# Gate/up of the experts as three fp32r products of split parts, and expert rows added to token rows in DRAM

## The chip, the cores and the metric

The kernel runs on one core of a Trainium2 chip. The time is device microseconds of one execution. PE is TensorE, DVE VectorE, ACT ScalarE, POOL GpSimd and SP SyncE, which issues most of the transfers.

## What is computed

Two layers of a trunk over 384 tokens (128 context, 256 latent) of 1024 features. The part that matters here is the mixture of experts at the end of each layer: each token picks 4 of 32 experts, and their outputs are added with its weights, beside one shared expert.

```python
def moe(h, lp):
    t = h.reshape(B * T, D)
    ...
    _, eidx = lax.top_k(masked, TOP_K)
    w = jnp.take_along_axis(scores, eidx, axis=-1)
    w = w / jnp.sum(w, axis=-1, keepdims=True) * ROUTE_SCALE
    combine = jnp.sum(jax.nn.one_hot(eidx, N_EXPERTS, dtype=jnp.float32) * w[..., None], axis=1)
    gu = jnp.einsum('nd,edf->nef', t, lp['w_exp_gu'])
    a = jax.nn.silu(gu[..., :EXPERT_FF]) * gu[..., EXPERT_FF:]
    a = (a * combine[..., None].astype(a.dtype)).reshape(-1, N_EXPERTS * EXPERT_FF)
    routed = a @ lp['w_exp_down'].reshape(N_EXPERTS * EXPERT_FF, D_MODEL)
    ...
    return (routed + shared).reshape(B, T, D)
```

Each expert has gate/up weights of 1024 x 512 (2 MB in fp32) and down weights of 256 x 1024 (1 MB).

## The kernel before

A layer runs through modulation, input projection, four mixers, gates and output projection, and then the experts. The large projections already use split parts (`project_split`, L1809): ACT writes a weight piece rounded to fp32r (L1001), DVE writes the rest (L1338, the piece minus its rounded part), and three fp32r products of 512 columns take the place of one fp32 product (L1822).

The experts work on tiles of CAP = 96 slots, one tile for each expert and further ones for experts with more than 96 tokens; with these inputs it is 32 tiles a layer, in 16 turns of two. Routing on DVE gives each of a token's four choices a slot; POOL scatters token numbers into a table in DRAM (L894) and reads it back. The token rows lie in DRAM (`token_rows`).

The loop has two slots, e = 0 and 1, and each engine runs its own `steps(turn)`; semaphores alone order them. PE's step for tile n (L2078): `gate_up` of tile n+1 (L2059, 8 fp32 products into one PSUM bank, through the helper line L1762), `turn_product` of tile n (L2013), `turn_gathered` of tile n+2 (L2052, eight transposes of gathered rows) and `down` of tile n (L2018, four fp32 products). ACT takes the SiLU (L1238), the transposed product (L1240), half of the transposed rows (L1244) and half of the output rows (L1248); DVE takes the product (L1669), the other half of the transposed rows (L1732) and of the output rows (L1735). The two slots' weights lie in W.

SP's step (L738): when `gate_up` has filled its bank, load the 2 MB of gate/up weights of tile n+3 into the slot just used; when `down` is done, load 1 MB of down weights of tile n+2; when both halves of the output rows are copied, write them to `y_slots` in DRAM (`write_rows`, L725). POOL's step (L916): when the rows of tile n+2 are transposed, copy the index column of tile n+4 (L904) and issue an indirect gather of its rows (L907).

After the loop POOL gathers, for each of a token's four choices, the rows of `y_slots` by slot (L927, twelve gathers of 128 rows a layer), DVE multiplies each by the token's weight and adds it to the shared expert's output `acc` (L1744), ACT takes the sum of squares and its root (`row_root`, L1173) and DVE the residual (`residual`, L1572). The slots of tiles that may not run are zeroed beforehand by POOL (L871, 96 x 16 rows of 4 KB).

Of the kernel before, what the change touches and what calls it, by code (L numbers as in the profile page):

```python
# [189 lines left out]
def plan_jobs():  # L190
# [100 lines left out]
    for i in range(2):  # L291
        for h in range(2):
            jobs.add(("xt", i, h), ("act", "dve")[h], BANK_XT + h)
# [17 lines left out]
STEP = (("gu", "dve"), ("aT", "act"), ("xt0", "act"), ("xt1", "dve"), ("y0", "act"), ("y1", "dve"))  # L311
TURN_JOBS, TURN_TAKEN = 2 * len(STEP), 6
# [37 lines left out]
def trunk(nc, a):  # L350

    J = JOBS
    with ExitStack() as ctx:
# [3 lines left out]
        def sb_twice(name, n):  # L357
# [54 lines left out]
                 "do_ready", "gate_ready", "merged_ready", "m_squared", "x_ready", "exp_ready", "chosen_ready", "slots_ready", "ones_ready", "gathers", "sp_steps", "sil_ready", "mod_params_in", "table_reset", "slots_out", "table_in", "rows_out", "tables_ready", "summed", "silu_ready",  # L412
                 "mod_used", "mod_rows_out", "modT_in", "lam_dots", "lam_exps", "head_normed", "mean_ready", "ret_squared", "branch_rs"]
        names += ["gates_in", "cache_out"] + [f"{n}{i}" for n in ("x_landed", "y_written", "index_copied") for i in range(2)]
        names += [f"y_landed{i}" for i in range(6)]
        names += ["dec_scaled", "mixture_rows", "post_root", "pre_root", "zeros_ready", "zeros_out", "halves_used", "high_ready", "low_ready", "h_split", "oT_high", "mgT_high"]
        landed_names = [f"piece_landed{i}" for i in range(RAW)] + ["gu_landed0", "gu_landed1", "dn_landed0", "dn_landed1"]
# [77 lines left out]
        xT = zf[:, 9728:9728 + 2 * KD * CAP].rearrange("p (s k n) -> p s k n", s=2, k=KD)  # L495
        yrow = zf[:, 11776:13824].rearrange("p (s n) -> p s n", s=2)
        ybuf = zf[:, 7680:13824].rearrange("p (s n) -> p s n", s=6)

        slot_f, weight, slot_u = vm[:, 1024:1036], vm[:, 1036:1048], vm[:, 1048:1060].bitcast(U32)
        token_f, token_u = vm[:, 1060:1063], vm[:, 1063:1066].bitcast(U32)  # L500
        tokens = vm[:, 1068:1068 + NT].bitcast(U32)
        index = vm[:, 1120:1122].bitcast(U32)
        expert_f, expert_u = vm[:, 1124:1124 + NT], vm[:, 1172:1172 + NT].bitcast(U32)
        turns_f, turns_u = vm[:, 1220:1221], vm[:, 1221:1222].bitcast(U32)
        ones = vm[:, 1232:1360]
# [29 lines left out]
        def expert_gu(s):  # L535
            return W[:, s * SLOT:(s + 1) * SLOT].rearrange("p (k n) -> p k n", k=KD)

# [132 lines left out]
        with nc.Fori(0, DEPTH) as l:  # L670
            with nc.Block() as block:

                @block.sync
                def _(sp):
# [24 lines left out]
                    def load_gate_up(s, src):  # L699
                        sp.dma_start(expert_gu(s), src.rearrange("(p k) n -> p k n", p=P)).then_inc(S[f"gu_landed{s}"], 16)  # L700
# [1446 lines left out]
```

## Time and profile before

| | us |
|---|---|
| median of 3 runs | 2185.84 (2184.77 to 2186.19) |
| the profiled execution | 2186.99 |
| its span | 2185.4 |
| PE busy in the span | 1951.3 (89%) |
| DVE busy | 832.7 (38%) |
| ACT busy | 628.2 (29%) |
| POOL busy | 318.8 (15%) |
| mean granted clock of PE | 0.953 of 2.4 GHz |

The profile is one execution. Matmuls overlap, so a busy PE is not a PE at its peak. DMA figures are those of the core's 16 DMA engines together: a share of 1 means that packets were in service on all of them all the time. The chain that ended last is 40% PE work, of which L1762 has 19% of the span and L1822 17%; DMA has 2%.

### The profile page before, as it was taken

The numbers are of one execution on the slowest core, as the hardware profiler recorded it, in microseconds if no ns is written. First come the engines' busy times: TensorE is split into PE (matmuls) and PEld (weight loads), VectorE is DVE, ScalarE is ACT, GpSimd is POOL, SyncE is SP. The second block draws the span as 40 slices with busy tenths as digits, with TensorE's granted clock in tenths as the row PEclk, the third lists the DMA queues.
The fourth block names the chain that finished last, engine by engine and source line by source line (L and its number), as shares of the span: only waits on it lengthen the run. The fifth ranks groups of instructions, "written<-read, shape, count | busy, mean of one in ns | idle before, by whom it ended". The sixth has DMA issues, their size and how long they took to land.

```text
span 2185.4 us, 24671 instructions
## 1 busy us (share of the span) xinstructions
PE 1951.3 (89%) x8272; PEld 1236.6 (57%) x8272; DVE 832.7 (38%) x1468; ACT 628.2 (29%) x1318; POOL 318.8 (15%) x381
## 2 busy tenths in 40 slices
PE   6998988999978999999169989989999789999990
PEld 3886656888753444444048866578887434444440
DVE  2345566444462111111523455664444521111115
ACT  3342357333340111111133423573232401111111
POOL 2004121300012011100210051223000121001102
PEclk9999998999999999999679999999999999999995
DMA  8442360734345999998375424617333569999974
GB/s 299 139 134 93 119 230 16 243 122 135 116 183 199 341 350 349 345 345 303 131 264 155 121 87 137 212 34 242 124 117 114 189 218 345 345 345 351 347 276 159
DMA packets 110956, 457.60 MB, mean 209 GB/s; under 512 B 11984, under 2 KB 19824, under 8 KB 87824
## 3 DMA queue, kind: packets, MB, share of 16 engines
q1 hardware_dynamic: 87168, 384.86, 50.7%
q0 software_dynamic: 20192, 65.15, 10.0%
q10 hardware_dynamic: 3504, 6.40, 0.8%
q8 instruction: 54, 0.88, 0.2%
q14 instruction: 38, 0.31, 0.0%
HBM read 411.69 MB, written 44.71 MB: 209 GB/s over the span
## 4 chain that ended last, share of the span: by engine, by line
PE 40%; DVE 4%; DMA 2%; ACT 2%; issue 1%; POOL 1%; SPq 0%; ACTq 0%; POOLq 0%; DVEq 0%
PE psum L1762 19%; PE psum L1822 17%; PE psum L1769 2%; PE psum L1787 1%; PE psum L2055 1%; DMA W<-in_w_mod 1%; POOL slot_tokens L894 1%; DVE W_split L1338 0%; DVE zf L1744 0%; DVE zf L1577 0%; DMA zf<-token_rows,vm 0%; DMA W<-in_w_in 0%; ACT hT L970 0%; DMA zf<-y_slots,vm 0%; PE psum L2015 0%
## 5 line engine op out<-in xcount | busy, mean ns | idle before, releaser
L1762 PE MATMUL psum<-W,zf 128*96 128x512 f32 (+1 forms) x1584 | 699.5, 597 | 9.5 <-issue 4.3
L1762 PEld LDWEIGHTS psum<-W,zf 128*96 128x96 f32 (+1 forms) x1584 | 254.3, 164 | 403.6 <-issue 388.8
L1822 PE MATMUL psum<-W_split,qT_split 128*128 128x512 f32 (+3 forms) x1536 | 405.7, 377 | 9.9 <-ACT hT L970 7.8
L1338 DVE TENSOR_TENSOR W_split<-W,W_split 128x2048 fp32r<-128x2048 f32 (+3 forms) x96 | 225.1, 2346 | 406.3 <-ACT W_split L1001 406.3
L1822 PEld LDWEIGHTS psum<-W_split,qT_split 128*128 128x128 f32 x1536 | 284.8, 190 | 60.3 <-ACT hT L970 8.6
L1001 ACT ACTIVATE W_split<-W 128x2048 fp32r<-128x2048 f32 (+3 forms) x96 | 176.0, 1839 | 414.6 <-PE psum L1822 343.0
L1822 PE MATMUL psum<-W_split,scratch_split 128*128 128x512 f32 x864 | 274.7, 390 | 0.6 <-DVE hT_split L1333 0.6
L1822 PE MATMUL psum<-W_split,hT_split 128*128 128x512 f32 x576 | 208.9, 390 | 5.8 <-DVE scratch_split L1536 5.8
L1669 DVE TENSOR_TENSOR zf<-psum,zf 96x256 f32<-96x256 f32 x64 | 26.9, 421 | 425.9 <-ACT zf L1238 410.3
L1822 PEld LDWEIGHTS psum<-W_split,scratch_split 128*128 128x128 f32 x864 | 161.6, 188 | 34.1 <-DVE hT_split L1333 0.8
L1822 PE MATMUL psum<-W_split,kT_split 128*128 128x512 f32 (+3 forms) x480 | 176.4, 367 | 0.0
L1238 ACT ACTIVATE zf<-psum 96x256 f32<-96x256 f32 x62 | 23.6, 380 | 494.7 <-PE psum L1762 494.7
L1787 PE MATMUL psum<-W,silT 128*32 128x512 f32 x384 | 66.5, 767 | 69.5 <-DMA W<-in_w_mod 69.4
L1822 PEld LDWEIGHTS psum<-W_split,hT_split 128*128 128x128 f32 x576 | 107.9, 188 | 28.8 <-DVE scratch_split L1536 6.3
L1735 DVE COPY zf<-psum 96x512 f32<-96x512 f32 x64 | 44.0, 687 | 201.4 <-PE psum L1762 201.4
L1822 PEld LDWEIGHTS psum<-W_split,kT_split 128*128 128x128 f32 x480 | 91.8, 191 | 13.3
L904 POOL COPY vm<-vm 96x1 uint32 (+1 forms) x64 | 11.5, 180 | 556.3 <-PE psum L2055 553.4
L1414 DVE TENSOR_REDUCE nmax<-psum 128x1 f32<-128x128 f32 (+1 forms) x144 | 64.6, 463 | 46.6 <-PE psum L1762 46.0
L1769 PE MATMUL psum<-const,zf 128*128 128x128 f32 x372 | 56.2, 292 | 29.1 <-DVE zf L1585 19.3
L1762 PE MATMUL psum<-kT,qT 64*128 64x384 f32 (+3 forms) x288 | 75.0, 485 | 5.1 <-DVE kT L1275 1.8
L877 POOL DMA_DIRECT2D kT<-mod_rows x8 | 4.4, 548 | 470.4 <-PE psum L1769 346.1
L1769 PEld LDWEIGHTS psum<-const,zf 128*128 128x128 f32 x372 | 47.2, 159 | 45.1 <-DVE zf L1585 20.2
(306 smaller groups left out, 2050.4 us busy)
## 6 DMA issues: line engine op xcount, KB each, us to landing
W<-in_w_exp_gu SPq DMA_DIRECT2D x64, 2048.0 KB, 9.8
W<-in_w_exp_down SPq DMA_DIRECT2D x64, 1024.0 KB, 8.6
W<-in_w_in SPq DMA_DIRECT2D x60, 1024.0 KB, 5.1
W<-in_w_mod SPq DMA_DIRECT2D x48, 1024.0 KB, 4.9
y_slots<-zf SPq DMA_DIRECT2D x64, 384.0 KB, 8.7
W<-in_w_br SPq DMA_DIRECT2D x16, 1024.0 KB, 5.1
y_slots<-kT POOLq DMA_DIRECT2D x2, 6144.0 KB, 33.6
W<-in_w_out SPq DMA_DIRECT2D x8, 1024.0 KB, 5.0
```

The source lines that it names most:

```text
L894: pool.indirect_dma_start(a["slot_tokens"], bass.IndirectOffsetOnAxis(ap=slot_u[:, i:i + 1], axis=0), token_u[:, i // TOPK:i // TOPK + 1], ...
L1001: nc.scalar.activation(high(j), piece(SPLITS[j]), ACT.Copy).then_inc(S["high_ready"], 1)
L1238: nc.scalar.activation(silu[0:CAP, 1 - e, :], psum[0:CAP, BANK_GU + 1 - e, 0:FF], ACT.Silu).then_inc(S["silu_ready"], 1)
L1338: V.tensor_tensor(piece(SPLITS[j], Wr), piece(SPLITS[j]), high(j).bitcast(F32), ALU.subtract).then_inc(S["low_ready"], 1)
L1414: V.tensor_reduce(nmax[:, col:col + 1], bank(key, P * len(keys_of(t))), AX, ALU.max, negate=True).then_inc(S["max_ready"], 1)
L1669: V.tensor_tensor(av[0:CAP, s], psum[0:CAP, gu, FF:2 * FF], silu[0:CAP, s], ALU.mult).then_inc(S["dve_emptied"], 1)
L1735: V.tensor_copy(yrow[0:CAP, e, C:], psum[0:CAP, BANK_Y + 1, :]).then_inc(S["dve_emptied"], 1)
L1762: ins = nc.tensor.matmul(dst, lhsT, rhs, start=(i == 0), stop=(i == len(pairs) - 1))
L1769: ins = nc.tensor.transpose(psum[0:n, J.bank(key), i * P:(i + 1) * P], src, ident)
L1787: ins = nc.tensor.matmul(bank(("mod", j), C, slice(32 * q, 32 * q + 32)), silTv[:, k, :], chunk, start=k == 0, stop=k == KD - 1)
L1822: ins = nc.tensor.matmul(bank(job, piece_size(key)[1]), act_part[:, k0 + k, t * P:(t + 1) * P], w_part[:, k, :], start=first and (k, i) == ...
L2055: ins = nc.tensor.transpose(psum[:, BANK_XT + h, k * CAP:(k + 1) * CAP], xg[0:CAP, s, (4 * h + k) * P:(4 * h + k + 1) * P], ident[0:CAP, 0 ...
```

## The change

Gate/up weights come in two halves of 1 MB, each with its own semaphore (`gu_landed` for slot and half). ACT rounds each half to fp32r into one of two buffers (`gate_up_high`, one for each half, shared by both slots), DVE overwrites the half in W with the rest, and PE multiplies rows and weights in three fp32r products for each of the 8 blocks of features. The gathered rows are split too: ACT writes both rounded halves of the transposed rows, DVE both rests. SP loads half 0 of a slot as soon as PE has used half 0, and half 1 at the end of `gate_up`. PE's order is unchanged: `gate_up` of the next tile, `turn_product`, `turn_gathered`, `down`.

The table in DRAM has two words for each slot, token number and weight; DVE's product multiplies by the slot's weight, so output rows leave the loop weighted. The shared expert's rows are written to `y_sums` in DRAM, and POOL adds each tile's 96 output rows to the rows of their tokens by an indirect transfer with addition, one tile after the other: it waits for each to land. Empty slots point to 96 rows behind the tokens'. After the loop SP loads `y_sums` back, and the roots and residuals follow; gathers and sums by choice are gone, and so is the zeroing of `y_slots`.

```diff
-STEP = (("gu", "dve"), ("aT", "act"), ("xt0", "act"), ("xt1", "dve"), ("y0", "act"), ("y1", "dve"))
+STEP = (("gu", "dve"), ("aT", "act"), ("xt0", "dve"), ("xt1", "dve"), ("y0", "act"), ("y1", "dve"))
+AHEAD = 8
...
+                    sp.wait_ge(*emptied(("y", "s", T - 1, 1)))
+                    sp.dma_start(a["y_sums"][0:T * P].rearrange("(t p) n -> p t n", p=P), acc).then_inc(S["shared_out"], 16)
...
                             if not (last and e == 1):
+                                sp.wait_ge(S["gu_half_used"], AHEAD + 2 + tile)
+                                weights = expert("w_exp_gu", expert_of(tile + 3))
+                                load_gate_up(1 - e, weights, (0,))
                                 sp.wait_ge(*job_filled(turn, e, "gu"))
-                                load_gate_up(1 - e, expert("w_exp_gu", expert_of(tile + 3)))
+                                sp.sem_inc(S["sp_steps"], 1)
+                                load_gate_up(1 - e, weights, (1,))
                             sp.wait_ge(*job_filled(turn, e, "y1"))
                             load_down(e, expert("w_exp_down", expert_of(tile + 2)))
-                            write_rows(turn, e)
...
+                    def add_rows(turn, e, less=(0, 0)):
+
+                        pool.wait_ge(*job_emptied(turn, e, "y0", less[0]))
+                        pool.sem_inc(S["gathers"], 1)
+                        pool.wait_ge(*job_emptied(turn, e, "y1", less[1]))
+                        pool.sem_inc(S["gathers"], 1)
+                        nc.gpsimd.tensor_copy(sum_index[0:CAP, e:e + 1], of_tile(turn * 2 + e, 0).bitcast(U32)).then_inc(S["sum_index_copied"], 1)
+                        pool.wait_ge(S["sum_index_copied"], turn * 2 + e + 1 + AHEAD)
+                        pool.sem_inc(S["gathers"], 1)
+                        pool.indirect_dma_start(a["y_sums"], bass.IndirectOffsetOnAxis(ap=sum_index[0:CAP, e:e + 1], axis=0),
+                                                yrow[0:CAP, e, :], None, compute_op=ALU.add).then_inc(S["y_added"], 16)
+                        pool.wait_ge(S["y_added"], turn * 32 + 16 * e + 16)
+                        pool.sem_inc(S["rows_added"], 1)
...
+                    def steps(turn, more, less=((0, 0), (0, 0))):
                         for e in range(2):
+                            if more != "none":
+                                pool.wait_ge(*job_filled(turn, e, "xt1"))
+                                if more == "rows":
+                                    gather(turn * 2 + e + 4, e, turn + 3)
+                                else:
+                                    pool.sem_inc(S["gathers"], 1)
+                                weights_of(turn * 2 + e + 2, e)
+                            add_rows(turn, e, less[e])
...
                     def steps(turn, last=False):
                         for e in range(2):
+                            if not last:
+                                act.wait_ge(S[f"gu_landed{e}0"], turn * 16 + 32 + 16 * e)
+                                act.wait_ge(S["gu_half_used"], turn * 2 + e + 2 + AHEAD)
+                                weights_high(e, 0)
...
+                                act.wait_ge(*job_filled(turn, e, "xt1"))
+                                rows_high(e)
+                                act.wait_ge(S[f"gu_landed{e}1"], turn * 16 + 32 + 16 * e)
+                                weights_high(e, 1)
                             act.wait_ge(*job_filled(turn, e, "y0", LESS["y"][e] if last else 0))
-                            act.wait_ge(S[f"y_written{e}"], turn * 16 + 16)
+                            act.wait_ge(S["rows_added"], turn * 2 + e - 1 + AHEAD)
...
+                    def weights_low(s, h, waited):
+                        dve.wait_ge(S["gu_high"], waited + h + 1)
+                        V.tensor_tensor(gate_up_half(s, h, Wr), gate_up_half(s, h), gate_up_high[h].bitcast(F32), ALU.subtract).then_inc(S["gu_low"], 1)
...
-                    for i in range(T * TOPK):
-                        dve.wait_ge(S[f"y_landed{i % 6}"], 16 * (i // 6 + 1))
-                        V.scalar_tensor_tensor(acc[:, i // TOPK], ybuf[:, i % 6], weight[:, i:i + 1], acc[:, i // TOPK], ALU.mult,
-                                               ALU.add).then_inc(S["summed"], 1)
...
+                    for t in range(T):
+                        residual(acc, 1, t)
...
+                    def gate_up(s, waited):
+
+                        for h in range(2):
+                            pe.wait_ge(S["gu_low"], waited + h + 1)
+                            parts = [(xT_split[a], (gate_up_high[h], gate_up_half(s, h, Wr))[b]) for a, b in ((0, 0), (0, 1), (1, 0))]
+                            for k in range(4):
+                                for i, (rows_part, w_part) in enumerate(parts):
+                                    ins = nc.tensor.matmul(psum[0:CAP, BANK_GU + s, :], rows_part[:, s, 4 * h + k, :], w_part[:, k, :],
+                                                           start=(h, k, i) == (0, 0, 0), stop=(h, k, i) == (1, 3, 2))
+                            ins.then_inc(S["gu_half_used" if h == 0 else "psum_filled"], 1)
```

## Rows read from the trace of the kernel before

**Rows 1.** The page, 40 equal slices of the span, busy share in tenths.
```profile
PE   6998988999978999999169989989999789999990
...
DMA  8442360734345999998375424617333569999974
```

**Rows 2.** Windows: us, each engine's busy us (count), granted clock, DMA share, GB/s.
```profile
11.00:16.00 5.00, 4.08 (x16) 0.43 (x16) 0.17 (x1) 4.66 (x8) 0.00 (x0) 1.00 1.01 418
403.00:437.00 34.00, 34.00 (x157) 28.29 (x156) 12.80 (x12) 10.46 (x11) 1.48 (x3) 1.00 0.90 299
1900.00:1990.00 90.00, 90.00 (x268) 38.28 (x268) 12.72 (x23) 12.15 (x30) 8.83 (x16) 1.00 1.01 346
1906.00:1910.00 4.00, 4.00 (x11) 1.52 (x10) 0.00 (x0) 0.00 (x0) 0.00 (x0) 1.00 1.01 282
1913.00:1917.00 4.00, 4.00 (x11) 1.50 (x10) 0.69 (x1) 0.59 (x1) 0.25 (x1) 1.00 1.00 375
1764.00:1786.00 22.00, 17.20 (x49) 7.58 (x50) 1.48 (x4) 1.38 (x4) 2.03 (x3) 0.85 0.46 150
2134.80:2172.10 37.30, 0.00 (x0) 0.00 (x0) 28.41 (x24) 5.62 (x10) 15.16 (x12) 0.56 0.53 179
```

**Rows 3.** Chain of waits, second layer: start us, us, what.
```profile
1180.13 98.26 PE psum L1822 x432
...
1809.01 10.53 PE psum L1762 x24
1819.54 0.20 PE psum L2015 x2
1819.74 0.66 PE psum L2055 x8
1820.40 10.44 PE psum L1762 x24
```

**Rows 4.** Groups by line and shape, whole run: busy us, mean ns, idle before.
```profile
L1338 DVE TENSOR_TENSOR W_split<-W,W_split 128x2048 fp32r<-128x2048 f32 x84 | 207.7, 2475 | 357.5 <-ACT W_split L1001 357.5
...
L1001 ACT ACTIVATE W_split<-W 128x2048 fp32r<-128x2048 f32 x84 | 161.1, 1925 | 339.1 <-PE psum L1822 304.5 <-DMA W<-in_w_in 20.4 <-DMA W<-in_w_br 14.2
...
L1244 ACT ACTIVATE zf<-psum 128x384 f32<-128x384 f32 x60 | 29.5, 491 | 0.0
```

**Rows 5.** DMA, 1900 to 1990 us: queues (packets, MB, share), gathers (median us to landing).
```profile
q1 hardware_dynamic: 3161, 28.02, 88.1%
q0 software_dynamic: 892, 3.14, 12.9%
...
zf<-token_rows,vm POOLq DMA_INDIRECT x8, 10.6
```

**Rows 6.** Timeline of POOL: one step of a gather.
```profile
1763.81 0.18 POOL L904 COPY vm<-vm 96x1 uint32<-96x1 uint32 x1 [2.99 <-PE psum L2055]
1764.80 0.92 POOL L907 DMA_INDIRECT zf<-token_rows,vm  x1 [0.80 <-POOL vm L904]
```

**Rows 7.** The tile token_rows: its transfers from issue to landing.
```profile
DMA to landing us min/median/max: 2.7/10.2/11.2
```

**Rows 8.** Timeline of the second layer's end.
```profile
2134.78 0.69 DVE L1735 COPY zf<-psum 96x512 f32<-96x512 f32 x1 [3.58 <-PE psum L1762]
...
2151.16 1.06 ACT L1173 ACTIVATE zf<-zf 128x1024 f32<-128x1024 f32 x1 [17.50 <-DVE zf L1744]
...
2153.62 0.29 ACT L1174 ACTIVATE rs<-stat,const 128x1 f32<-128x1 f32 x1
...
2154.51 0.16 DVE L1576 RECIPROCAL rs<-rs 128x1 f32<-128x1 f32 x1
...
2156.03 1.22 DVE L1578 TENSOR_TENSOR x<-x,zf 128x1024 f32<-128x1024 f32 x1
...
2170.83 1.22 DVE L1578 TENSOR_TENSOR x<-x,zf 128x1024 f32<-128x1024 f32 x1
```

**Rows 9.** DMA issues of the whole run: KB each, median us to landing.
```profile
x<-in_x_prompt ACTq DMA_DIRECT2D x1, 512.0 KB, 3.9
```

More of the change, by code:

```diff
@@ L750, in _ @@
                     steps(turns - 2, last=True)
-                    for e in range(2):
-                        write_rows(turns - 1, e, (LESS["act"][e], LESS["dve"][e]))
+                    sp.wait_ge(S["rows_added"], turns * 2 + AHEAD)
+                    sp.sem_inc(S["sp_steps"], 1)
+                    for t in range(T):
+                        sp.dma_start(acc[:, t], a["y_sums"][t * P:(t + 1) * P, :]).then_inc(S[f"y_landed{t}"], 16)
                 @block.gpsimd
@@ L870, in _ @@
                     pool.wait_ge(S["zeros_ready"], 1)
-                    pool.dma_start(a["y_slots"].rearrange("(p i) n -> p i n", i=NT)[:, NE:, :],
-                                   zero_row[0:CAP, None, :].to_broadcast([CAP, NT - NE, D])).then_inc(S["zeros_out"], 16)
+                    for name in ("token_rows", "y_sums"):
+                        pool.dma_start(a[name][T * P:, :], zero_row[0:CAP]).then_inc(S["zeros_out"], 16)
                     def fetch_gates(n):
@@ L901, in gather @@
                     def gather(tile, e, n):
[L903 to L904 removed]
+                        nc.gpsimd.tensor_copy(index[0:CAP, e:e + 1], of_tile(tile, 0).bitcast(U32)).then_inc(S[f"index_copied{e}"], 1)
                         pool.wait_ge(S[f"index_copied{e}"], n)
@@ L2020, in down @@
                                  ).then_inc(S["psum_filled"], 1)
-                    pe.wait_ge(S["gu_landed1"], 16)
+                    for h in range(2):
+                        pe.wait_ge(S[f"gu_landed1{h}"], 16)
                     def shared_gate_up(t):
@@ L2080, in steps @@
                             before = previous(turn, e)
-                            gone = (1 if last and e == 1 else 0)
+                            gone = (2 if last and e == 1 else 0)
                             if not (last and e == 1):
@@ L2093, in steps @@
                                 turn_gathered(e)
-                            pe.wait_ge(*job_emptied(turn, e, "aT", LESS["act_aT"][e] if last else 0))
+                            pe.wait_ge(*job_emptied(turn, e, "aT"))
                             pe.wait_ge(S[f"dn_landed{e}"], turn * 16 + 16 * (e + 1))
-                            pe.wait_ge(*job_emptied(*before, "y0", gone))
+                            pe.wait_ge(*job_emptied(*before, "y0"))
                             down(BANK_Y, aT[:, e], e, 0, CAP)
```

171 lines of the change are left out of this document (99 added, 72 removed).

## Prediction

> **What bounds the kernel now.** I read the page by slices first [rows 1]: PE is at 9 tenths in both expert loops (slices 14 to 18 and 34 to 38 of 40), DMA is at 9 tenths in the same slices, and nowhere else do both stand at 9 for long. The windows say it sharper [rows 2]: in 1900 to 1990 us PE is busy 90.00 of 90.00 us at a granted clock of 1.00 (the 2.4 GHz level), DVE 12.72 and ACT 12.15 us, and the DMA share is 1.01 at 346 GB/s. The chain of waits [rows 3] gives the tile: 24 records of L1762 in 10.53 us (8 of `down`, then 16 of `gate_up`: an fp32 product of 512 columns is two records of 0.44 us), 0.20 us for `turn_product`, 0.66 us for `turn_gathered`, and the next group 11.39 us later (11.30 from the other slot), 11.35 us on average. PE waits for nothing in the loop, so PE sets the pace. But the second resource has no room: a tile moves 2.10 MB of gate/up weights, 1.05 MB of down weights, 0.39 MB of gathered rows and 0.39 MB of written rows, 3.93 MB, and 3.93 MB in 11.35 us is the 346 GB/s of the window. The engines can do better when only weight loads run (418 GB/s in 11 to 16 us), and do worse while gathered rows are mixed in (282 GB/s in 1906 to 1910, against 375 in 1913 to 1917) [rows 2]. So shortening PE's part of a tile helps only as far as DMA can follow.
>
> **Gate/up in three products.** Removed: 16 records, 16 x 0.44 = 7.0 us. Added: 24 fp32r matmuls of 512 columns. The projections of the mixers run this form: 432 in 98.26 us, 0.227 us each [rows 3]. 24 x 0.227 = 5.5 us, so PE's tile would be 11.35 - 1.55 = 9.8 us. The stationary tile has 96 instead of 128 columns; I take no difference.
>
> The parts must be made. ACT copies two halves of 128x2048 (1.925 us each) and one more row copy (0.49), DVE subtracts two halves (2.475 each) and one more row half (about the same half microsecond) [rows 4]. Per tile ACT now has 12.15 x 11.35/90 = 1.5 us and DVE 1.6 us [rows 2], so they come to 5.9 and 7.1 us; both fit beside a tile of 9.8 us. Their latency is on the path once per half, since one high buffer per half serves both slots: from the end of `gate_up` of one tile, half 1 of the next needs `turn_product` and `turn_gathered` (0.86), two row copies (0.98), the high part (1.93) and the low part (2.48), 6.3 us before waits, while PE does the transposes (0.86), `down` (3.5) and half 0 (2.7), 7.1 us. That just hides; if it didn't, the excess would be added to each tile (a lower bound of about 10.0 us for a tile, by my estimate of some 0.1 us for each hand-over). Cover gone, the price is 1 us a tile for each us of delay. Before the loop the first splits stand beside the wait for the tables and the gathered rows; the larger table, the two extra DVE operations and the row split cost about a microsecond a layer, the first and last `gate_up` give about as much back: zero, 3 us either way.
>
> **Rows added in DRAM.** Removed from each tile: SP's write of 0.39 MB. Added: a POOL issue of the same size that adds to rows of y_sums. No row shows an adding transfer. As a plain write it would change nothing, since those bytes still leave the core; less than nothing it could cost only if POOL's queue moved rows faster than SP's, and it doesn't. In 1900 to 1990 the write's queue moved 28.02 MB in 88.1% of the window, 353 GB/s, and POOL's queue, which holds the gathers alone, 3.14 MB in 12.9%, 270 GB/s [rows 5]. The write is then worth 1.1 us of all engines and a gather 1.46 us. An add must fetch the token's row, as a gather does, and write one, as the write does: 2.57 us, 1.46 more than now. In bytes: 0.39 MB more, 4.32 MB a tile, at 346 GB/s 12.5 us. The upper end: the mixed rate. At 282 mixed and 375 unmixed, 11.35 us for 3.93 MB holds 3.5 us of mixing a tile; POOL's queue would carry three times as much (0.39 gathered, 0.79 for the add), 10.5 us at 282 and the last 1.36 MB at 375: 14.1 us. The lower end: all 4.32 MB at the 418 GB/s of pure loads, 10.3 us. I take 12.5, the value by the loop's own rate, since the loop is the nearest row.
>
> The window shows the share at 1.01 with nothing to spare, so a second read per added byte must lengthen the tile [rows 2]. The Trainium skill has a rule that speaks against the change here (Collectives: The Full Stack, The bandwidth ceiling: the fold count and why AG ≠ RS ≠ AR): a transfer that adds costs twice a copy, because it reads two sources on the same ring, and the addition itself is free. By that rule the add is two reads and the tile 12.5 us; by the write's row alone it is a copy and the tile stays at 11.35 us or less. No run here shows which.
>
> The new waits. POOL waits for each add to land (`y_added`) before anything else. Behind that wait stand the next gather and the next weight copy; PE's `turn_gathered` and DVE's product wait for those, and ACT's and DVE's copies into yrow wait for `rows_added` of two tiles before. A POOL step is: index copy 0.18, 0.80 of wait, gather issue 0.92 [rows 6], weight copy 0.2, index copy and wait 1.0, then issue to landing of the add. Gathers land after 10.6 us in the loaded loop [rows 5] and 2.7 us at best [rows 7], so a step is 3.1 + 2.7 = 5.8 to 3.1 + 10.6 = 13.7 us. In a 12.5 us tile it decides from a landing of 9.4 us on. Weight packets of half the size let POOL's rows in more often, so I keep it just below, and as a rival. SP loses the waits for y0 and y1 and its write, and issues half 0 of the weights some 2.7 us sooner; both only fill the same engines earlier.
>
> Full steps with loads behind them are about 28 a layer (the first ones start with DMA at a share of 0.46 [rows 2], the last three load nothing), 56 in all: 56 x (12.5 - 11.35) = +64 us.
>
> **The end of a layer.** From the last yrow copy (2134.78) to the last residual (2172.05) are 37.3 us: write, twelve gathers through POOL, twelve weighted sums on DVE [rows 8]. After: copy 0.7, POOL 1.0, add 5 (between a gather's best 2.7 [rows 7] and twice that; nearer the second, as it reads and writes), hand-over 0.5 by my estimate, a 512 KB load 3.9 [rows 9], root 2.8 (2151.16 to 2153.91), three residuals of 2.74 (2154.51 to 2157.25), 8.2: 22 us [rows 8]. That is 15 saved; an earlier add still ahead of it would leave 8; I take 13, 26 in both layers. The zero fill of y_slots (6 MB a layer) goes too; it lay beside PE's projections, busy 34.00 of 34.00 us from 403 to 437 [rows 2], so I give it nothing. The 1.5 MB of shared rows written to y_sums fall in the stretch with a DMA share of 0.46 [rows 2]: nothing, and 4 us at 375 GB/s a layer if that cover is gone.
>
> **Sum.** The profiled execution took 2186.99 us (span 2185.4, and 1.6 around it); the median of the runs, 2185.84, is 1.15 lower. 2187 + 64 - 26 = 2225, as a median 2224 us. The rivals below start from the median. The change breaks even at a tile of 11.35 + 26/56 = 11.8 us.
>
> **Rivals.** B, faster: DMA follows. For it: 418 GB/s without gathered rows; halves issued earlier keep the queue from running dry; a share of 1.01 may hide packets that merely wait. Against: 9.8 us would need 441 GB/s counted with two reads, more than [rows 2] has anywhere; even with the add as a plain write it needs 401. Tiles of 10.3 us give 2186 + 56 x (-1.05) - 26 = 2101; PE's and the splits' own 10.0 us 2084; the end of it is 11.8 us, 2185.
>
> C, slower still: POOL's serial order decides. The add stands in POOL's queue behind a gather issued 2 us before, so its landing holds what is left of that one too. At a landing of 10.6 us the tile is 13.7: 2186 + 56 x 2.35 - 20 = 2298. For it: the loaded landing of 10.6 [rows 5]. Against: 2.7 at best [rows 7], smaller weight packets, and a longer tile unloads the engines. At the mixed rate's 14.1 us: 2186 + 154 - 20 = 2320.
>
> D, PE waits so long in each tile that its clock falls to the lower level, 1.2 GHz: PE's part doubles to 19.6 us, some 2620 us. The clock was 0.56 in the layer's end, when PE did nothing for 37 us, but 1.00 through the loop [rows 2]; waits of 2 to 3 us per tile are far from the former. That three products aren't shorter than one (the change not doing what it says) has 432 matmuls against it [rows 3]; with DMA as the bound it would hardly move the time, and stands in the forecast.
>
> **Chances.** Forecast A (tile of 11.8 to 13.3 us, 2185 to 2270): 0.48. B: 0.36. C: 0.13. D: 0.03. Range 2095 to 2310: it reaches into B down to a tile of 10.2 us and into C past its 2298, leaving out about 0.1 below and 0.1 above. A's own range is 2185 to 2270. A measurement of this kernel can tell some 0.2%, 4.4 us, from no change; around the break-even tile that is 0.08 us either way, 0.04. So faster 0.35, same 0.04, slower 0.61.
>
> **What would show it.** In the loop: DMA share still at 1, PE below 90% with idle time ended by DVE's low parts or ACT's copies that in turn wait for a load or for `rows_added`; tile period near 12.5; the fp32r records at 0.227 us; POOL's adds landing in 8 to 9 us, bytes per tile 4.3 MB. PE busy 100% with a share below 1 would prove B; POOL idle only for `y_added` with a share well below 1 would prove C. In the layer's end: some 24 us instead of 37. Wrong it would be above all if an adding packet takes no longer than a plain one, or far longer than a gather and a write together.

## The result, and the profile after

| | kernel before | changed kernel |
|---|---|---|
| median of the runs, us | 2186.02 (2184.77 to 2188.36) | 2227.52 (2225.41 to 2232.79) |
| profiled execution / its span, us | 2186.99 / 2185.4 | 2226.58 / 2225.0 |
| a tile, mean of 30 between copies into yrow, us | 11.35 | 12.44 |
| last copy into yrow to last residual, us | 37.3 | 26.0 |

The changed kernel is slower by 1.8%: 1.0184 times the time of before, 95% interval 1.0165 to 1.0202. The forecast was 2224 us. The time came out as forecast, and most terms of the sum did too; the mechanism under the largest term was another, the one I had kept as rival C. That is the subject of the experiments.

First the page of the changed kernel (the slices that answer to [rows 1], the chain that ended last).

```profile
PE   6998988999977888898469989889998778888883
...
DMA  8442461433367999999475424514432589999994
...
PE psum L1900 16%; DMA y_sums<-zf,vm 10%; PE psum L1840 4%; PE psum L2145 2%; PE psum L1847 2%; PE psum L1865 1%; DMA W<-in_w_mod 1%; POOL slot_tokens L908 1%; POOL vm L938 1%; DMA zf<-token_rows,vm 0%; DVE W_split L1400 0%; POOL vm L920 0%
```

In the expert loops (slices 14 to 19 and 34 to 39) PE has fallen from 9 tenths to 8, but for one slice; DMA still stands at 9. And a transfer that did not exist before, `y_sums<-zf`, the adding of rows, holds 10% of the chain, second only to the mixers' projections. A window in the second loop gives the sizes (columns as in [rows 2]).

```profile
1800.00:2000.00 200.00, 170.21 (x673) 101.15 (x674) 105.01 (x98) 92.05 (x113) 48.44 (x75) 0.96 0.96 314
```

The DMA queues and issues of the same window (columns as in [rows 5]):

```profile
q1 hardware_dynamic: 7097, 51.72, 71.3%
q0 software_dynamic: 3136, 11.01, 24.7%
...
zf<-token_rows,vm POOLq DMA_INDIRECT x15, 7.8
y_sums<-zf,vm POOLq DMA_INDIRECT x15, 9.2
```

PE is busy 85% of the window. The DMA engines, nearly full by their share of 0.96, move 314 GB/s, less than the 346 of [rows 2]; an add lands after 9.2 us. What sets the pace, then? POOL's timeline shows one of its turns (start, us, engine, line; in brackets the idle time before and what ended it):

```profile
1896.50 1.46 POOL L931 DMA_INDIRECT y_sums<-zf,vm  x1 [0.83 <-POOL vm L928]
1907.08 0.18 POOL L938 COPY vm<-vm 96x1 uint32 x1 [9.12 <-DMA y_sums<-zf,vm]
1908.06 0.95 POOL L941 DMA_INDIRECT zf<-token_rows,vm  x1 [0.80 <-POOL vm L938]
1909.02 0.20 POOL L920 COPY vm<-vm 96x1 f32 x1
1909.14 0.18 POOL L928 COPY vm<-vm 96x1 uint32 x1
1910.15 1.46 POOL L931 DMA_INDIRECT y_sums<-zf,vm  x1 [0.83 <-POOL vm L928]
```

The chain of waits in the same stretch consists of these long pieces (start, us, what):

```profile
1896.50 10.24 DMA y_sums<-zf,vm
...
1910.15 8.98 DMA y_sums<-zf,vm
...
1922.83 9.21 DMA y_sums<-zf,vm
```

An add is issued at 1896.50 and lands 10.24 us later; only then do the index copy, the gather, the copy of the weights (L920) and the next add's index copy run, and the next add goes out 3.4 us after the landing. The next turns are 12.7 and 12.6 us long. POOL does little in a turn and is nevertheless what the tile waits for. The waits of 1800 to 2000 us (engine and line, what it waited for, us in total, times, longest) show how that reaches the others:

```profile
POOL vm L938 <- DMA y_sums<-zf,vm: 90.9, 11, 9.5
ACT qT_split L1273 <- PE psum L2145: 84.8, 16, 8.0
DVE W_split L1796 <- ACT qT_split L1273: 50.4, 17, 5.0
DVE zf L1733 <- POOL vm L920: 46.6, 13, 5.2
...
PE psum L2145 <- DVE hT_split L1792: 27.7, 13, 3.6
```

DVE's product (L1733) waits for the weights that POOL copies behind the landing; the split of the gathered rows (L1792) stands behind the product on DVE; PE's gate/up (L2145) waits for the split.

The timeline of the second layer's end, to be held against [rows 8]:

```profile
2191.78 0.69 DVE L1819 COPY zf<-psum 96x512 f32<-96x512 f32 x1 [3.77 <-PE psum L1840]
...
2195.23 1.81 POOL L928 COPY vm<-vm 96x1 uint32 x1 [4.56 <-DMA y_sums<-zf,vm]
2197.83 1.42 POOL L931 DMA_INDIRECT y_sums<-zf,vm  x1 [0.79 <-POOL vm L928]
2203.32 1.28 SPq L766 DMA_DIRECT2D zf<-y_sums  x3
2206.88 1.06 ACT L1213 ACTIVATE zf<-zf 128x1024 f32<-128x1024 f32 x1 [16.22 <-DMA zf<-y_sums]
...
2216.55 1.23 DVE L1640 TENSOR_TENSOR x<-x,zf 128x1024 f32<-128x1024 f32 x1
```

The last add waits 2.8 us for the one before it (landed about 2195.2), then lands in 5.4 us, the loads of the sums follow: 26.0 us in all.

The whole difference of the spans, 39.6 us, taken apart at the first and the last copy into yrow and at the last residual of each layer: the loops +34.0 and +32.2, the ends -11.3 and -11.3, the way to the first copy +5.9 in the first layer and -3.7 in the second, and -6.1 after the last residual. Together +39.7.

### The profile page after: what moved, and what is told of

Its sections match the earlier page's. It is cut to its first block, busy times and chain, and to the rows that moved or that the text cites. A ratio compares the mean times of both kernels' runs of the same rounds, so it can differ in the third digit from the quotient of the medians.

```text
span 2225.0 us, 27059 instructions
## 1 busy us (share of the span) xinstructions
PE 1916.1 (86%) x8784; PEld 1336.2 (60%) x8784; DVE 1112.1 (50%) x1640; ACT 888.7 (40%) x1510; POOL 441.3 (20%) x551
## 4 chain that ended last, share of the span: by engine, by line
PE 26%; DMA 12%; issue 4%; DVE 4%; ACT 2%; POOL 2%; POOLq 1%; DVEq 0%; SPq 0%; ACTq 0%
PE psum L1900 16%; DMA y_sums<-zf,vm 10%; PE psum L1840 4%; PE psum L2145 2%; PE psum L1847 2%; PE psum L1865 1%; DMA W<-in_w_mod 1%; POOL slot_tokens L908 1%; POOL vm L938 1%; DMA zf<-token_rows,vm 0%; DVE W_split L1400 0%; POOL vm L920 0%; DVE zf L1639 0%; DVE x L1640 0%; DMA W<-in_w_in 0%
## 5 line engine op out<-in xcount | busy, mean ns | idle before, releaser
L2145 PE MATMUL psum<-qT_split,hT_split 128*96 128x512 f32 x512 | 204.9, 465 | 108.3 <-DVE hT_split L1792 101.8
L1840 PE MATMUL psum<-W,zf 128*96 128x512 f32 (+1 forms) x560 | 256.8, 601 | 5.4 <-ACT zf L1264 2.9
L1273 ACT ACTIVATE qT_split<-W 128x2048 fp32r<-128x2048 f32 x64 | 122.6, 1915 | 344.2 <-PE psum L2145 340.6
L1796 DVE TENSOR_TENSOR W_split<-W,qT_split 128x2048 fp32r<-128x2048 f32 x64 | 146.7, 2292 | 188.1 <-ACT qT_split L1273 188.1
L2145 PE MATMUL psum<-W_split,hT_split 128*96 128x512 f32 x512 | 216.0, 422 | 0.0
L2145 PEld LDWEIGHTS psum<-qT_split,hT_split 128*96 128x96 f32 x512 | 96.0, 187 | 194.9 <-issue 157.2
L2145 PE MATMUL psum<-scratch_split,hT_split 128*96 128x512 f32 x512 | 173.1, 399 | 0.0
L1840 PEld LDWEIGHTS psum<-W,zf 128*96 128x96 f32 (+1 forms) x560 | 86.9, 165 | 125.2 <-issue 109.2
L1796 DVE TENSOR_TENSOR W_split<-W,scratch_split 128x2048 fp32r<-128x2048 f32 x64 | 145.9, 2280 | 7.3 <-ACT scratch_split L1273 7.3
L1733 DVE SCALAR_TENSOR_TENSOR zf<-psum,vm,zf 96x256 f32<-96x256 f32 x64 | 30.7, 479 | 186.8 <-POOL vm L920 178.5
L1273 ACT ACTIVATE scratch_split<-W 128x2048 fp32r<-128x2048 f32 x64 | 122.3, 1911 | 0.0
L2145 PEld LDWEIGHTS psum<-W_split,hT_split 128*96 128x96 f32 x512 | 91.2, 178 | 38.7 <-issue 3.6
```

The lines of the kernel that those rows point to most:

```text
L1273: nc.scalar.activation(gate_up_high[h], gate_up_half(s, h), ACT.Copy).then_inc(S["gu_high"], 1)
L1733: V.scalar_tensor_tensor(av[0:CAP, s], psum[0:CAP, gu, FF:2 * FF], slot_weight[0:CAP, s:s + 1], silu[0:CAP, s], ALU.mult, ALU.mult).then_i ...
L1796: V.tensor_tensor(gate_up_half(s, h, Wr), gate_up_half(s, h), gate_up_high[h].bitcast(F32), ALU.subtract).then_inc(S["gu_low"], 1)
L1840: ins = nc.tensor.matmul(dst, lhsT, rhs, start=(i == 0), stop=(i == len(pairs) - 1))
L2145: ins = nc.tensor.matmul(psum[0:CAP, BANK_GU + s, :], rows_part[:, s, 4 * h + k, :], w_part[:, k, :], start=(h, k, i) == (0, 0, 0), stop=( ...
```

## The experiments

Two theories stood against each other. Bytes: a second read for each added byte fills the DMA engines (the forecast's reason). POOL's order: the wait for the add to land, with the next gather and the copies queued behind it (rival C). "Tile" below is always the mean of the 30 intervals from the first copy into yrow to the last but one, two layers together; in the changed kernel, e5 and e7 the middle of the loop is 0.3 to 0.6 us longer. Landings are medians from issue to landing, between 1800 and 2000 us.

| kernel | time, us | against before, 95% interval | tile, us | DMA share, 1800 to 2000 | landing of an add, us |
|---|---|---|---|---|---|
| before | 2186.0 | | 11.35 | | |
| changed | 2227.5 | 1.017 to 1.020 | 12.44 | 0.96 | 9.2 |
| e1_split_only | 2130.5 | 0.972 to 0.978 | 10.34 | 1.02 | none |
| e2_add_only | 2218.2 | 1.013 to 1.019 | 12.2 (two stretches, see below) | 0.98 | 8.3 |
| e3_late_wait | 2137.1 | 0.977 to 0.980 | 11.0 | 1.03 | 9.0 |
| e4_plain_write | 2132.0 | 0.973 to 0.980 | 11.0 | 0.97 | 6.9 |
| e5_dve_weights | 2269.1 | 1.035 to 1.042 | 13.0 | 0.87 | 9.3 |
| e6_eighth_down | 2125.8 (single execution) | | 10.75 | 0.96 | 6.6 |
| e7_after_skip | 2224.4 | 1.015 to 1.020 | 12.3 | 0.85 | 8.9 |
| e8_late_skip | 2130.9 | 0.973 to 0.978 | 10.9 | 0.93 | 9.1 |
| e9_down_after_gu | 2145.1 | 0.979 to 0.982 | 11.05 | 1.02 | 8.3 |
| e10_down_after_gu_skip | 2130.7 | 0.972 to 0.975 | 10.9 | 0.93 | 8.7 |

**e1: the split alone.** The kernel before with the parts of the diff that split gate/up (ACT's high parts, DVE's low parts, half loads, 24 products), and y_slots as it was.

```diff
-            jobs.add(("xt", i, h), ("act", "dve")[h], BANK_XT + h)
+            jobs.add(("xt", i, h), "dve", BANK_XT + h)
...
-                                load_gate_up(1 - e, expert("w_exp_gu", expert_of(tile + 3)))
+                                load_gate_up(1 - e, weights, (0,))
...
+                                load_gate_up(1 - e, weights, (1,))
```

> The kernel before with gate/up in three fp32r products, and the expert rows written to their slots and gathered at the end as before. Bytes as the bound: the tile still moves 3.93 MB; by the prices of before (10.0 us of weights, written rows among them, and 1.46 of gathers, 11.4 us of all engines) it stays near 11.0 to 11.4 us, so 2160 to 2190 us, DMA share at 1.0 and PE busy below 95% in the loop. If bytes do not bind: the tile falls to PE's and the splits' 9.8 to 10.2 us, so 2186 - 56 x 1.4 = 2108 us, 2095 to 2125, share still near 1.0. If the split's chain over ACT and DVE is what makes the tile of the changed kernel 12.8 us: 12 us or more, 2220 us or more.

The window of e1 (columns as in [rows 2]), and one `gate_up` in its chain of waits:

```profile
1800.00:2000.00 200.00, 194.05 (x816) 118.53 (x814) 122.03 (x114) 107.89 (x134) 47.44 (x38) 1.00 1.02 377
```

```profile
1878.52 5.58 PE psum L2123 x24
```

2130.5 us, tile 10.34. It lies between the first two cases, nearer to the second. The same bytes that took 11.35 us a tile before now pass in 10.34, at 377 GB/s with the share at 1.02. So the 346 GB/s of [rows 2] were PE's pace and not what the engines could carry, although the share stood at 1.01 there as well. At this pace the loads do decide: in the chain of waits from 1850 to 1900 us, gate/up loads are 70%. This half of the change is worth 56 us (against the 2186.9 us of before on the same chip).

**e2: the adding alone.** The changed kernel with gate/up as in the kernel before.

```diff
-                            load_gate_up(1 - e, weights, (0,))
...
-                            load_gate_up(1 - e, weights, (1,))
+                            load_gate_up(1 - e, expert("w_exp_gu", expert_of(tile + 3)))
```

> The kernel before with the rows added in DRAM, gate/up as one fp32 product from one 2 MB load. Bytes: 3.93 MB and the second read of the add, as in the changed kernel, so a tile of 12.3 to 12.8 us: 2186 + 56 x 1.2 - 26 = 2227 us, 2200 to 2235, DMA share 0.95 or more. POOL's order: landing of an add (9.0 us in the changed kernel) plus 3.4 to 3.7 us of POOL's own steps, also 12.4 to 12.8 us. PE alone (the adds hidden): 11.35 us, 2186 - 26 = 2160 us. Only that last one speaks for the split as the cause of the longer tile.

2218.2 us, tile 12.2: the split is not the cause of the longer tile. The mean hides two stretches, and they tell the two theories apart, though both had expected the same mean tile. The first 19 intervals of the first layer and the first 13 of the second are 11.3 or 11.4 us, the tile of the kernel before; after them most are 12 to 15 us. Two windows of the first layer, one from each stretch (columns as in [rows 2]), and the waits of DVE's product in the first and in the second:

```profile
707.00:915.00 208.00, 208.00 (x622) 88.93 (x621) 30.03 (x55) 29.07 (x72) 51.18 (x87) 1.00 1.01 344
930.00:1060.00 130.00, 117.11 (x324) 48.05 (x322) 15.86 (x30) 15.86 (x39) 28.01 (x48) 0.93 0.86 280
```

```profile
DVE zf L1696 <- ACT zf L1263: 118.7, 18, 6.6
```

```profile
DVE zf L1696 <- POOL vm L905: 101.6, 9, 13.5
```

In the first stretch every tile's rows are added in DRAM, PE is busy all the time, and the tile is no longer than without adds. An adding transfer alone therefore does not lengthen the tile, as bytes needed it to. In the second the tiles are longer while fewer bytes move and the share is lower, and the product waits for POOL's copy of the weights nine times in ten. An add lands in 7.8 us in the first window and in 10.0 in the second; with the 3.4 us from a landing to the next add, the first makes 11.2 us, just under PE's 11.35, and the second 13.4. Why the landing grows on the way is open.

**e3: the wait moved.** Nothing else than the place of the wait: the next add still goes out only when the one before has landed, but the gather and the three small copies around it no longer stand behind it. (The first turn is written out ahead of the loop, since the first add has nothing to wait for.)

```diff
                         pool.sem_inc(S["gathers"], 1)
+                        if not (isinstance(turn, int) and turn * 2 + e == 0):
+                            pool.wait_ge(S["y_added"], turn * 32 + 16 * e)
+                            pool.sem_inc(S["rows_added"], 1)
                         pool.indirect_dma_start(a["y_sums"], ...
-                        pool.wait_ge(S["y_added"], turn * 32 + 16 * e + 16)
-                        pool.sem_inc(S["rows_added"], 1)
```

> The changed kernel with POOL's wait for an add moved from right behind its issue to right ahead of the next add's issue, so that the gather and the two copies between no longer stand behind it. POOL's order as the bound: the tile falls to the larger of landing + 1 (10 us) and the split's own 10 to 11 us, so 2227 - 56 x 2.3 = 2098 us, 2080 to 2130, and POOL idles less. Bytes as the bound: the share can only rise from 0.96 to 1.0, so the tile stays at 12.3 to 12.8 us, 2199 to 2228 us, and the landing of an add grows instead (above 10 us).

The window of e3, its DMA queues and its waits:

```profile
1800.00:2000.00 200.00, 181.61 (x737) 108.84 (x738) 115.82 (x108) 98.78 (x126) 110.17 (x89) 0.98 1.03 350
```

```profile
q1 hardware_dynamic: 7720, 56.18, 74.3%
q0 software_dynamic: 3969, 13.92, 28.4%
```

```profile
ACT qT_split L1277 <- DMA W<-in_w_exp_gu: 95.8, 17, 5.9
DVE W_split L1800 <- ACT qT_split L1277: 85.0, 18, 5.4
...
POOL y_sums L934 <- DMA y_sums<-zf,vm: 2.5, 2, 1.3
```

2137.1 us: 90 us of the changed kernel were this wait, and the same bytes fit into 11.0 us a tile. POOL now waits 2.5 us of 200 for an add, although adds land no sooner (9.0). Bytes had forecast 2199 or more, and fell. POOL's order had 2080 to 2130, a little too low, because behind POOL's wait the next limit stands at once: the share is 1.03, and ACT's splits now wait for gate/up loads. That the wait stays at all has a reason that no run here shows: by the Trainium skill (DMA: Bandwidth & Descriptors, Rules for kernel authors) an adding transfer reads its destination and writes it later, and what another writes there in between is lost.

**e4: a plain write in place of the add.** The sum over a token's experts is left out.

```diff
-                                                yrow[0:CAP, e, :], None, compute_op=ALU.add).then_inc(S["y_added"], 16)
+                                                yrow[0:CAP, e, :], None).then_inc(S["y_added"], 16)
```

> The changed kernel with its add replaced by a plain write of the same rows to the same addresses, so the sum over a token's experts is left out and the rest stays. Bytes: if an add costs a second read, that read (1.0 to 1.46 us of all engines a tile) goes and the tile falls to 11.4 to 11.8 us: 2227 - 56 x 1.2 = 2160 us, 2145 to 2175. If an add costs what a write costs: the same time, 2220 to 2232 us. POOL's order: the tile falls by as much as the landing does (9.0 us with the add); both theories then differ only in the share, which stays near 0.95 for bytes and falls below 0.9 for POOL's order.

POOL's queue and the landing of the written rows in e4:

```profile
q0 software_dynamic: 3821, 13.42, 21.8%
...
y_sums<-zf,vm POOLq DMA_INDIRECT x18, 6.9
```

2132.0 us: faster than bytes had it, and slower than a landing 2.3 us shorter would make it in full (2227 - 56 x 2.3 = 2098). The share stayed at 0.97, as bytes had it, and the time is what neither had, so the run doesn't tell the two apart, but it gives the price of adding. In the trace's packet records from 1800 to 2000 us, an adding row of 4 KB takes 320 to 329 ns (1338 of POOL's 2688 row packets in the changed kernel, 1728 of 3397 in e3); here hardly a packet takes that (42 of 3276), and 1682 take 150 to 159 ns, against some 430 in the two others: an adding row costs about twice a plain one. By the queue's share a tile's transfers of POOL cost e3 3.2 us of all engines (28.4% of 200 us over 17.7 tiles, 13.92 MB by 0.786) and this kernel 2.55 (43.6 us over 17.1). With 1.3 to 1.46 of them for the gather (e1's 12.6% and [rows 5]), an add is 1.75 to 1.9 us and the plain write 1.1 to 1.25. Straight from the packets, 96 rows of 0.327 us over 16 engines, the add is 1.96 us.

The Trainium skill's rule that the prediction weighed (Collectives: The Full Stack, The bandwidth ceiling: the fold count and why AG ≠ RS ≠ AR), an adding transfer costs twice a copy, agrees with these packets, at 325 to 155 ns. The page tells it of the ring steps of collectives; for a kernel's own adding transfer these packets are the evidence. But it is not what made the kernel slower.

**e5: the weights' copy taken from POOL.** DVE copies a tile's weights itself, right ahead of the product; POOL's wait stays.

```diff
-                        nc.gpsimd.tensor_copy(slot_weight[0:CAP, e:e + 1], of_tile(tile, 1)).then_inc(S["weight_copied"], 1)
...
+                        V.tensor_copy(slot_weight[0:CAP, s:s + 1], weight).then_inc(S["weight_copied"], 1)
                         dve.wait_ge(S["silu_ready"], n)
```

> The changed kernel with the copy of a tile's weights taken out of POOL's queue and given to DVE right ahead of the product; POOL still waits for each add before the next gather. If POOL's cycle itself is the bound (an add's landing of 9.0 us and then index copy, gather, index copy, add issue, 3 us): the tile stays at 12.2 to 12.8 us, 2195 to 2227 us. If POOL's wait reaches the other engines only through the weight copy (DVE's product waited for it 13 times in 200 us of the changed kernel, up to 5.2 us): the tile falls to the 11.1 us of the kernel with the late wait, 2130 to 2150 us.

The waits of e5 from 1800 to 2000 us, and a turn of POOL on its timeline:

```profile
POOL vm L935 <- DMA y_sums<-zf,vm: 96.1, 12, 9.3
...
PE psum L2133 <- DMA zf<-token_rows,vm: 34.2, 12, 6.7
```

```profile
1891.92 1.46 POOL L928 DMA_INDIRECT y_sums<-zf,vm  x1 [0.83 <-POOL vm L925]
1901.72 0.54 POOL L935 COPY vm<-vm 96x1 uint32 x1 [8.34 <-DMA y_sums<-zf,vm]
1903.07 0.95 POOL L938 DMA_INDIRECT zf<-token_rows,vm  x1 [0.80 <-POOL vm L935]
1904.02 0.20 POOL L925 COPY vm<-vm 96x1 uint32 x1
1905.04 1.46 POOL L928 DMA_INDIRECT y_sums<-zf,vm  x1 [0.83 <-POOL vm L925]
```

2269.1 us, where I had 2195 to 2227 by POOL's order and 2130 to 2150 by the weights' copy alone. The second falls: with that copy gone, PE waits for gathered rows, which POOL also issues behind the landing, and POOL's turn (9.5 us of landing, 3.6 of steps, 13.1) is the tile as before. It was one turn, not one copy. That it became 0.5 us longer than in the changed kernel I can trace only in part: in the window the landing is 9.3 instead of 9.2, and the index copy has a median of 0.54 us instead of 0.18. Such a copy is long where DVE's subtraction of a weight half runs beside it: the row at 1901.72 ends 0.04 us after that subtraction (1899.93, 2.29 us long). The loops are 31 us longer than in the changed kernel and the two ends together 12, with two adds still ahead of the second layer's last one instead of one. The rest stays open.

**e6: fewer bytes loaded.** Only an eighth of each down load is issued in the loop; the other down weights stay what they were, so 7/8 of the down weights are left out.

```diff
-                            load_down(e, expert("w_exp_down", expert_of(tile + 2)))
+                            w_down = expert("w_exp_down", expert_of(tile + 2)).rearrange("(p k) n -> p k n", p=P)
+                            sp.dma_start(expert_dn(e)[:, 0:1, 0:256], w_down[:, 0:1, 0:256]).then_inc(S[f"dn_landed{e}"], 16)
```

> The changed kernel with an eighth of each down load in the loop (the rest of the down weights is left out and the old ones stay in place): 0.92 MB less a tile, share of the engines about 0.75. POOL's order: the tile stays landing + 3.5 to 3.8 us at whatever landing this load gives, between 5.4 (the layer's last add, alone) and 9.0 us; with 7.0 it is 10.7 us, 2227 - 56 x 2.1 = 2110 us, and PE still waits. If the landing is the add's own and not the load's: 9.0 us and 2210 us or more. Bytes: 12.8 - 2.5 = 10.3 us, about 2090 us, at a share still near 0.95.

The window of e6 and its queues:

```profile
1800.00:2000.00 200.00, 188.59 (x764) 110.07 (x764) 119.07 (x113) 105.03 (x130) 66.48 (x95) 1.00 0.96 279
```

```profile
q1 hardware_dynamic: 7990, 41.68, 62.0%
q0 software_dynamic: 4035, 14.17, 33.6%
```

2125.8 us in a single execution. The landing fell from 9.2 to 6.6 us: it depends on the loads beside it. The tile of 10.75 is POOL's 6.6 + 3.8 and 0.35 more; the wait for an add is down to 12.9 us in 200, from 90.9, so POOL's order has all but stopped deciding. But the share, expected at 0.75, stayed at 0.96, with only 279 GB/s moved. POOL's rows now take 3.7 us of all engines a tile (67.2 us over 18.0 tiles) instead of e3's 3.2, and the eighth of the down loads travels in 2304 packets of 1 KB, which hold 6% of the window for 2.4 MB. A share near 1 does not mean that no more bytes could pass.

**e7: half of the rows left out, the wait kept.** A tile has 96 rows, and those that stand for no token carry an index past the last token; gathers and adds now leave them out.

```diff
-                                                yrow[0:CAP, e, :], None, compute_op=ALU.add).then_inc(S["y_added"], 16)
+                                                yrow[0:CAP, e, :], None, bounds_check=T * P - 1, oob_is_err=False, compute_op=ALU.add)...
...
+                                                bounds_check=T * P - 1, oob_is_err=False).then_inc(S[f"x_landed{e}"], 16)
```

> The changed kernel whose gathers and adds leave out the rows of a tile that stand for no token (index past the last token), about half of 96; the wait for each add stays. POOL's order: the tile is landing + 3.5 to 3.8 us; with half the packets the landing falls to between 5.4 and 7.5 us, so 9.8 (PE's and the splits' own pace) to 11.2 us: 2227 - 56 x 2.3 = 2098 us, 2060 to 2140. Bytes: some 1.6 us a tile less of all engines, 11.2 us at best from the changed kernel's 12.8, 2137 us, share still 0.95.

The window of e7, then POOL's queue and the landing of its adds:

```profile
1800.00:2000.00 200.00, 171.85 (x676) 101.93 (x674) 106.33 (x98) 92.97 (x115) 48.65 (x75) 0.96 0.85 284
```

```profile
q0 software_dynamic: 3182, 5.47, 12.2%
...
y_sums<-zf,vm POOLq DMA_INDIRECT x15, 8.9
```

2224.4 us against 2227.5, the intervals of the two ratios overlap. Half of POOL's bytes and half of their engine time are gone (11.01 to 5.47 MB, 24.7% to 12.2%), the share has fallen to 0.85, and nothing is won. With the first stretch of e2 this is the sharpest blow to bytes as the cause. For POOL's order I had expected a shorter landing; it stayed at 8.9 us, and so did the tile, as that theory needs. Why a landing with half the rows lasts as long is open: there are as many packets (3182 and 3136), small ones of 4 and 8 bytes standing in place of the rows left out.

**e8: the same with the late wait.** e3 with the edit of e7.

> The kernel with the late wait (2137 us, tile 11.1 us at a share of 1.03) with the rows that stand for no token left out of gathers and adds. Bytes as its bound: some 1.6 us a tile of POOL's queue go (half of 3.2), so the tile falls to 9.8 to 10.2 us, where PE and the splits stand: 2137 - 56 x 1.1 = 2075 us, 2060 to 2100, PE above 95% busy in the loop. If it is not bytes that bind there: 2137 us, no change.

2130.9 us, tile 10.9, share 0.93: 6 us less than e3 instead of the 62 expected, and even these are not clear of noise (the intervals of the two ratios overlap). So the bytes of POOL's rows are not what holds e3 at 11.0 either, or only by 0.1 us.

**e9 and e10: down loads behind the gate/up loads.** In e3 ACT waited for gate/up loads, in front of which SP had issued a down load needed much later. Both kernels turn that order round (e9 from e3, e10 from e8).

```diff
+                            if not (first and e == 0):
+                                sp.wait_ge(*job_filled(*previous(turn, e), "y1"))
+                                load_down(1 - e, expert("w_exp_down", expert_of(tile + 1)))
-                            sp.wait_ge(*job_filled(turn, e, "y1"))
-                            load_down(e, expert("w_exp_down", expert_of(tile + 2)))
...
```

> The kernel with the late wait (tile 11.1 us, DMA share 1.03, ACT waiting for gate/up loads that land after 12.7 us) with SP's down load of a tile issued behind the gate/up loads that it stood ahead of. Bytes as the bound: with the share at 1.03 the order of the loads changes nothing, 2130 to 2145 us, landing of gate/up shorter and of down longer by as much. Order of the loads as the bound: gate/up lands 2 to 3 us sooner and the tile falls to 10.2 to 10.6 us, 2085 to 2110 us.

> The same edit on the late wait with the rows that stand for no token left out (2131 us, tile 11.1 us, share only 0.93). Order of the loads as the bound: the engines have 0.07 of room, the tile falls to 10.2 to 10.4 us, 2080 to 2105 us. If what holds that kernel is neither: unchanged, 2125 to 2137 us.

The landings of the loads in e9, and the new wait of PE:

```profile
W<-in_w_exp_gu SPq DMA_DIRECT2D x36, 1024.0 KB, 8.1
W<-in_w_exp_down SPq DMA_DIRECT2D x18, 1024.0 KB, 11.3
```

```profile
PE psum L1848 <- DMA W<-in_w_exp_down: 18.2, 17, 1.3
```

The window of e10 (columns as in [rows 2]):

```profile
1800.00:2000.00 200.00, 186.65 (x777) 113.54 (x776) 119.14 (x110) 104.38 (x128) 60.94 (x92) 1.00 0.93 328
```

Gate/up lands 4.6 us sooner than in e3 (8.1 against 12.7), and PE waits for down loads instead; 2145.1 us, at the upper end of what bytes had for it and 8 us more than e3, within the overlap of the two intervals. e10 is at 2130.7 us what e8 was. The order of the loads is not the limit. What holds these kernels between 10.8 and 11.1 us, where e1 has 10.34 and PE and the splits need 9.8, is not settled: in e9 a share of 1.02 speaks for the DMA engines, in e10 the share is 0.93 and PE is busy 93% (186.65 of 200 us), so that neither is full. e1's 10.34 and the second read of an add, 0.65 to 1.0 us, would make e3's 11.0; but e8 leaves half of POOL's rows out and stays at 10.9.

Of the kernels that still compute the whole result, five beat the kernel before: e1, e3, e8, e9 and e10, by 2.0 to 2.6%. e1 gains it in the loop and keeps the long end (36.6 us a layer); the others give part of the loop back and have ends of about 25 us.

## Why the prediction was right, and where it was not

**Gate/up in three products: right.** 24 records were put at 5.5 us; in e1 they run in 5.58. ACT's 5.9 and DVE's 7.1 us a tile came out as 6.0 and 7.1 (46.55 and 55.17 us in the 100 us from 1800 on, by 12.8 us, the tile in the middle of the loop). That the chain of splits hides behind PE holds in e1, with PE busy 194 of 200 us and a tile of 10.34, 0.5 above the 9.8.

**The price of an add: right in kind, too high in size.** 2.57 us of all engines were put down for it, 1.75 to 1.96 were measured. The plain write in it, 1.1, was right (1.1 to 1.25); the second read is 0.65 (3.2 less 2.55, e3 and e4) to 1.0 (96 rows of 0.327 less 0.159 us over 16 engines), and not the 1.46 of a gather.

**Bytes as the bound: this is the step that failed.** 4.32 MB at 346 GB/s gave 12.5 us. In e3 the same transfers pass in 11.0 us, and in the first stretch of e2 in 11.35. (The profile counts an added row once: a tile of the changed kernel shows 3.9 MB, not the 4.3 that the forecast named as its sign.) The error was to read a share of 1.01 beside a PE of 100% as "nothing to spare" and to take the rate of that window for the engines' limit. The rate was what PE asked for: e1 has 377 GB/s at 1.02, and e6 shows 0.96 at 279 GB/s. The Trainium skill warns of this reading (Perfetto Trace Analysis, Identifying the Most-Contended Engine): for DMA, go by the HBM utilization, which is throughput against the peak, and not by occupancy, which sixteen engines make misleading. These two windows agree with it. Rival B said it ("a share of 1.01 may hide packets that merely wait") and had 10.0 to 11.8 us for it; without POOL's wait the changed kernel would have ended there, in B and faster than before.

**POOL's serial order: named, priced, and put on the wrong side.** The prediction had the list of what stands behind the wait, 3.1 us of POOL's steps and a landing between 2.7 and 10.6. Measured are 3.4 us and 9.2. What failed is the comparison: the step was held against 12.5 us and found "just below" with a deciding landing of 9.4. Against the 11.0 us in which the transfers pass in e3, 3.4 + 9.2 = 12.6 decides by far. That "weight packets of half the size let POOL's rows in more often" no run shows: with 2 MB loads, in the stretches of e2 where POOL decides, an add lands in 9.3 us (1960 to 2150) and 10.0 us (930 to 1060), with halves in 9.2.

**The sum: right, by two errors that met.** 12.5 us came from bytes that aren't the bound, and 12.6 us from an order that is; that the two meet is luck. The loop was put at +64 and came to +66.2; the ends at -26 and came to -22.6; the rest at zero and came to -3.9. The forecast's test for C, POOL idle only for `y_added` with a share well below 1, was half met by the changed kernel itself (POOL idle, share 0.96) and fully by e7 (0.85).

**The end of a layer: right but for one term.** 24 us were forecast, 26.0 measured. The add lands in 5.4 us there (5 forecast) and a 512 KB load in 4.4 (3.9). The add still ahead, which the prediction named, costs 2.8 us of waiting, and POOL's index copy takes 1.8 us instead of 0.2, ending with a DVE operation beside it.

**Small ones.** The way to the first copy, put at zero to 3 us, costs 5.9 in the first layer (4.3 of it in e1, so most of it is the split) and gains 3.7 in the second, where e1 loses 3.3. So what came with the adding gains some 7 us there; whether it is the zero fill that is gone wasn't tried. The 6.1 us after the last residual I had not counted, and no run explains them. Rival D didn't come: the granted clock is 0.96 in the window, not half.

## What to carry to other kernels

A DMA share near 1 beside a full compute engine says that packets are under way, not that the queues could carry no more: find the rate in a stretch where transfers alone set the pace, or keep both readings with a chance each. When a change adds a wait to an in-order engine, add up that engine's whole turn (landing and every instruction behind the wait) and compare it with each other bound, not only with the one you believe in. And a wait for a transfer belongs right ahead of the next instruction that needs it: moving this one past four instructions was worth 90 us, 4%.

## What the hardware showed that I had not expected

An adding row packet of 4 KB takes 320 to 329 ns, a plainly written one 150 to 159. Leaving out half of a transfer's rows halved its bytes and its engine time (24.7% to 12.2%), and left its landing at 8.9 us beside weight loads; an eighth of the down loads in place of all of them brought it to 6.6, and with no loads beside it, at a layer's end, it is 5.4.

POOL's copies of 96 words mostly take 0.2 us. In the twelve kernels together 479 of them take more than 0.3 us, up to 2.7, and 466 of these end within 0.05 us after a DVE operation of 128x2048 elements that ran beside them (mostly the splits' subtraction). In the kernel before, whose loop has no such operation, none of 64 is long. In e3 the weights' copy takes 2.2 us on average.
